# Residual rows summed in memory by an accumulating scatter, and the first norm taken tile by tile, in a hybrid encoder step on one core

## The chip, the cores and the metric

The kernel runs on one core of one Trainium2 chip. The metric is device time in microseconds (us) of one execution, the median of several runs. Times inside an execution are counted from the start of the span, which runs from the first to the last instruction that the profiler records.

## The reference

One layer of a streaming encoder is applied to 304 tokens: 16 meta tokens and 256 prompt tokens (one stream) and 32 sample tokens (another stream). All data are float32, rows have 2048 elements. What matters here:

```python
x = x + mix @ w_out                      # the mixer (RG-LRU and mLSTM branches), on rmsnorm(x)
xf = rmsnorm(x)                          # 304 rows of 2048
g_idx = argmax(xf @ w_rg + b_rg)         # one of 4 groups for each token
top_v, top_i = top_k(e_logits[g_idx], 2) # two of its 4 experts; top_w: softmax times p(group)
for e in range(16):
    hdn = silu(xf @ w_g[e]) * (xf @ w_u[e])           # 2048 -> 512
    out = out + gates[:, e:e + 1] * (hdn @ w_d[e])    # 512 -> 2048
y = rmsnorm(x + out)
```

## The kernel before

**Start.** Five DMAs issued by ScalarE (`load_x`) bring x into three tiles of up to 128 tokens: meta tokens and the first 112 prompt rows (tile 0), 128 prompt rows (tile 1), the last 16 prompt rows and the 32 sample rows (tile 2, 48 rows). All five count on one semaphore `x_loaded`; SyncE (which then starts to stream weights) and ScalarE (which then squares the tiles, L1003) wait for all five. VectorE turns the sums into means, ScalarE takes the root (L1006), VectorE scales the tiles (L1370), TensorE turns them (L659, L650), ScalarE and VectorE split them into a rounded part and its rest (L1017, L1380), and TensorE begins the first of 104 products with slices of `w_in` (L665 to L667). Ahead of it TensorE runs `WARM` matmuls (L655), whose results nothing reads. Every weight matrix is split into a rounded part (ScalarE, L1011) and a rest (VectorE, L1375), and a product is three matmuls for each of its steps.

**Routing.** After the mixer, x with its residual stands in `xtok`, the normed rows are stored in memory (`xn2_rows`). VectorE chooses experts and gives each (token, expert) a slot: each expert has 64 slots (`CAP`), filled from the first one, and 16 experts make 1024 slots, one round. GpSimd scatters each token's number into `slot_token` at its two slots (L1976); the table was filled with zeros at the start, so that an empty slot names token 0.

**Expert loop.** It runs over eight pairs of experts (the first partly ahead of the loop, the last behind it). Weights come in units of 2 MB into a ring of four slots, issued by SyncE when TensorE has finished with a slot (`groups_done`); ScalarE rounds them (L1237), VectorE takes the rest (L1788), TensorE multiplies (L904, L905, and L931 to L933 for the down product). GpSimd's function `store` does for each pair, in this order: the index column of the next pair's slots (`gidx`, L1994), the gather of their rows (L1996), then for each of the two experts a wait for its result and its store into `slot_out` (L2005). It waits for both stores, frees `ysb`, and goes on to the next pair. VectorE copies a result out of PSUM in four pieces (`results_out`, L1818).

**End.** When all is stored, GpSimd gathers for each of the three tiles its two result rows per token (L2020, six gathers). VectorE multiplies them by the weights `w1` and `w2` and adds them to x (`take`, L1875 and L1878), ScalarE squares (L1326) and takes the root (L1328), VectorE scales (`scaled`, L1889), SyncE stores the outputs (L604).

```python
v.wait_ge(groups_done, p(12, G_MOE + s + 1))    # results_out
if e == 0:
    v.wait_ge(y_free, p(1, 1))
```

## Time and profile before

| | us |
|---|---|
| median of three runs | 1998.38 (1995.9 to 1998.81) |
| profiled execution, its own time | 2001.61 |
| its span | 2000.1 |
| mean granted clock of TensorE | 0.976 of full speed |
| busy: TensorE, VectorE, ScalarE, GpSimd | 1879.3, 1241.1, 1005.1, 100.9 |

The busy times are sums over the whole span; the stages have different limits, so the rows below are taken from single stages. In a timeline a row gives the start and the length of an instruction (of several, where a count stands behind it), and in square brackets how long its engine had been idle before it and what ended that. Matmuls are pipelined, so their ends are modelled.

### The profile page before, as it was taken

What the parts mean: (1) busy time and instruction counts of PE and PEld (TensorE: products, weight loads), DVE (VectorE), ACT (ScalarE), POOL (GpSimd) and SP (SyncE); (2) the same over time, 40 slices, a digit from 0 to 9 for tenths busy, and PEclk for the clock granted to TensorE, in tenths of its full rate; (3) what the DMA queues carried; (4) which work ended last, traced back from release to release, by engine and by line L of the source; (5) the groups of instructions that cost most, each with busy time, mean ns of one, the idle gap of its engine ahead of it and who ended that gap; (6) DMA issues with size and microseconds to landing.
All of it is one profiled execution on the core that took longest, in us unless ns stands there. A gap on an engine that the chain in (4) does not pass through costs nothing.

```text
span 2000.1 us, 28137 instructions
## 1 busy us (share of the span) xinstructions
PE 1879.3 (94%) x11723; PEld 1679.6 (84%) x11723; DVE 1241.1 (62%) x1437; ACT 1005.1 (50%) x999; POOL 100.9 (5%) x188
## 2 busy tenths in 40 slices
PE   6999999999999999999999999999988989898981
PEld 5999999999999999999999999998666666666650
DVE  4764634547645445664343445444799999999984
ACT  5333644653334433453334333333678787878761
POOL 3001011000000000000000000000100000000001
PEclk8999999999999999999999999999999999999996
DMA  6555554545444444445565675546599999999975
GB/s 165 160 155 139 148 143 126 144 128 146 121 123 132 118 133 132 122 119 166 150 166 150 171 194 159 157 127 240 230 375 421 399 411 398 419 394 410 402 305 157
DMA packets 379167, 422.83 MB, mean 211 GB/s; under 512 B 13823, under 2 KB 358747, under 8 KB 362969
## 3 DMA queue, kind: packets, MB, share of 16 engines
q1 hardware_dynamic: 369849, 385.55, 59.0%
q0 software_dynamic: 7504, 29.75, 4.2%
q10 hardware_dynamic: 1712, 6.04, 1.0%
q8 instruction: 80, 1.31, 0.3%
q14 instruction: 22, 0.18, 0.0%
HBM read 405.87 MB, written 15.45 MB: 211 GB/s over the span
## 4 chain that ended last, share of the span: by engine, by line
PE 79%; DMA 10%; DVE 5%; issue 3%; ACT 3%; ACTq 0%; POOL 0%; DVEq 0%; POOLq 0%; SPq 0%
PE bank L629 17%; PE bank L631 16%; PE bank L630 16%; DMA ring<-in_w_exp_gate 5%; DMA ring<-in_w_exp_down 4%; PE bank L931 3%; PE bank L932 3%; PE bank L933 3%; PE bank L685 3%; PE bank L789 2%; PE bank L791 2%; PE bank L790 2%; ACT w_high L1237 1%; DVE w_low L1788 1%; PE bank L737 1%
## 5 line engine op out<-in xcount | busy, mean ns | idle before, releaser
L1375 DVE TENSOR_TENSOR low<-ring,high 128x2048 fp32r<-128x2048 f32 x172 | 394.1, 2291 | 566.0 <-ACT high L1011 565.7
L629 PE MATMUL bank<-x_high,high 128*128 128x304 f32 x2160 | 662.6, 307 | 0.0
L631 PE MATMUL bank<-x_high,low 128*128 128x304 f32 x2160 | 652.0, 302 | 0.0
L1011 ACT ACTIVATE high<-ring 128x2048 fp32r<-128x2048 f32 x172 | 329.1, 1913 | 533.5 <-DMA ring<-in_w_in 317.8
L630 PE MATMUL bank<-x_low,high 128*128 128x304 f32 x1904 | 572.1, 300 | 0.0
L1788 DVE TENSOR_TENSOR w_low<-ring,w_high 128x2048 fp32r<-128x2048 f32 x192 | 430.8, 2284 | 22.2 <-ACT w_high L1237 21.4
L1237 ACT ACTIVATE w_high<-ring 128x2048 fp32r<-128x2048 f32 x192 | 363.3, 1922 | 98.0 <-DMA ring<-in_w_exp_gate 33.5
L629 PEld LDWEIGHTS bank<-x_high,high 128*128 128x128 f32 x2160 | 405.9, 188 | 5.0 <-issue 3.3
L631 PEld LDWEIGHTS bank<-x_high,low 128*128 128x128 f32 x2160 | 406.1, 188 | 0.0
L630 PEld LDWEIGHTS bank<-x_low,high 128*128 128x128 f32 x1904 | 358.5, 188 | 1.4
L904 PE MATMUL bank<-w_high,xs 128*128 128x512 f32 x512 | 210.5, 411 | 28.1 <-DVE xs L1799 12.4
L905 PE MATMUL bank<-w_low,xs 128*128 128x512 f32 x512 | 202.3, 395 | 0.0
L904 PEld LDWEIGHTS bank<-w_high,xs 128*128 128x128 f32 x512 | 97.2, 190 | 72.3 <-DVE w_low L1788 34.6
L630 PE MATMUL bank<-hb_rounded,high 128*128 128x304 f32 x512 | 154.8, 302 | 0.0
L931 PE MATMUL bank<-w_high,hs_high 128*64 128x512 f32 x256 | 104.8, 409 | 25.8 <-DVE hs_low L1810 25.8
L905 PEld LDWEIGHTS bank<-w_low,xs 128*128 128x128 f32 x512 | 97.4, 190 | 18.4
L932 PE MATMUL bank<-w_high,hs_low 128*64 128x512 f32 x256 | 104.2, 407 | 0.0
L933 PE MATMUL bank<-w_low,hs_high 128*64 128x512 f32 x256 | 103.9, 406 | 0.0
L630 PEld LDWEIGHTS bank<-hb_rounded,high 128*128 128x128 f32 x512 | 96.3, 188 | 0.0
L931 PEld LDWEIGHTS bank<-w_high,hs_high 128*64 128x64 f32 x256 | 35.9, 140 | 57.0 <-issue 35.3
L629 PE MATMUL bank<-ym_high,high 128*128 128x304 f32 x256 | 77.7, 303 | 0.0
L631 PE MATMUL bank<-ym_high,low 128*128 128x304 f32 x256 | 77.5, 303 | 0.0
(372 smaller groups left out, 2145.3 us busy)
## 6 DMA issues: line engine op xcount, KB each, us to landing
ring<-in_w_in SPq DMA_DIRECT2D x120, 1024.0 KB, 5.6
ring<-in_w_exp_gate SPq DMA_DIRECT2D x32, 2048.0 KB, 9.2
ring<-in_w_exp_up SPq DMA_DIRECT2D x32, 2048.0 KB, 10.9
ring<-in_w_exp_down SPq DMA_DIRECT2D x32, 2048.0 KB, 11.0
ring<-in_w_proj_rnn SPq DMA_DIRECT2D x20, 1024.0 KB, 6.1
ring<-in_w_proj_mlstm SPq DMA_DIRECT2D x16, 1024.0 KB, 6.1
ring<-in_w_out SPq DMA_DIRECT2D x16, 1024.0 KB, 6.1
slot_out<-HB POOLq DMA_DIRECT2D x16, 512.0 KB, 8.4
```

The costliest lines, as they stand in the source:

```text
L629: pe.matmul(dst, hi[:, k, :], rhs_high(k), start=(k == 0), stop=False)
L630: pe.matmul(dst, hi[:, k, :], rhs_low(k), start=False, stop=False)
L631: last = pe.matmul(dst, lo[:, k, :], rhs_high(k), start=False, stop=(k == KD - 1))
L904: pe.matmul(dst, xs[:, kk, e, :], w_hi[:, k, :], start=(kk == 0), stop=False)
L905: last = pe.matmul(dst, xs[:, kk, e, :], w_lo[:, k, :], start=False, stop=(kk == KD - 1))
L931: pe.matmul(dst, h_hi, w_hi[:, b, :], start=(k == 0), stop=False)
L932: pe.matmul(dst, h_lo, w_hi[:, b, :], start=False, stop=False)
L933: last = pe.matmul(dst, h_hi, w_lo[:, b, :], start=False, stop=(k == KE - 1))
L1011: act.activation(high[n % 4], raw[n % 4], ACT.Copy).then_inc(t_split, 1)
L1237: act.activation(w_high[(2 * q + c) % 4], half(w_raw[s % 4], c), ACT.Copy).then_inc(w_split, 1)
L1375: v.tensor_tensor(low[n % 4], raw[n % 4], high[n % 4].bitcast(F32), ALU.subtract).then_inc(t_rest, 1)
L1788: v.tensor_tensor(half(w_low[s % 4], c), half(w_raw[s % 4], c), w_high[(2 * q + c) % 4].bitcast(F32), ALU.subtract).then_inc(w_rest, 1)
```

## The change

Two things are changed together.

The first is where the experts' results are summed. x is stored in memory (`x_rows`) by SyncE once the mixer is done. The slot table gets a second word: beside the token's number its weight, so its scatters wait until VectorE has made `w1` and `w2`. Empty slots name token 304, which is out of bounds, and gathers and scatters leave such rows out. In the loop GpSimd loads, behind the gather of the next pair, the index and weight column of the pair at hand (`sidx`). VectorE multiplies each result by its weight as it takes it out of PSUM, for which it waits until `sidx` is there. GpSimd adds the rows of a result to `x_rows` by an indirect DMA that accumulates; the second expert's add waits until the first one's is done. At the end SyncE loads the three tiles of `x_rows` back; the six gathers and the six multiply-adds are gone.

The second is the start. Each tile of x has its own semaphore, and ScalarE squares a tile when it has landed. A root on a word that nothing reads stands ahead of the squares. `WARM` goes from 24 to 8, and 2, 2 and 6 matmuls whose results nothing reads follow the transposes of the three tiles.

The diff, without the declarations of semaphores:

```diff
     xn2_rows = nc.dram_tensor("xn2_rows", (T, DM), F32)
-    slot_token = nc.dram_tensor("slot_token", (SLOTS + P, 1), I32)
-    slot_out = nc.dram_tensor("slot_out", (SLOTS, DM), F32)
+    slot_token = nc.dram_tensor("slot_token", (SLOTS + P, 2), I32)
+    x_rows = nc.dram_tensor("x_rows", (T, DM), F32)
     ctx = ExitStack()
...
         kc = sb("kc", [P, NE + EG])
-        tokid = sb("tokid", [P, 3], I32)
+        tokw = sb("tokw", [P, 2, 3, 2], I32)
+        tokw_f = tokw[:, :, :, :].bitcast(F32)
+        sidx = sb("sidx", [CAP, 2, 2], I32)
+        sidx_f = sidx[:, :, :].bitcast(F32)
         nrounds = sb("nrounds", [P, 2], I32)
         slot_i = sb("slot_i", [P, 2, 3], I32)
-        gidx = sb("gidx", [P, 1], I32)
+        gidx = sb("gidx", [P, 2], I32)
         SQ_GROUPS = [(0, 4), (4, 8), (8, 12), (12, 14), (14, 16)]
...
         diag8 = sb("diag8", [NH, 2 * NH])[:, :]
-        zeros_i = sb("zeros_i", [P, (SLOTS + P) // P], I32)
+        no_token = HBf[:, 2 * BW + 4 * P:2 * BW + 4 * P + (SLOTS + P) // P * 2].bitcast(I32)
         x2t = [AB[:, :, :].rearrange("p a b -> p (a b)")[:, j * T:(j + 1) * T] for j in range(4)]
...
         y1 = xntok
-        y2 = HBf[:, 0:HALF].rearrange("p (a b) -> p a b", a=3)
         nbf = OGf[:, DM:2 * DM]
...
         NVEC, NPAR = 11, 3
-        WARM = 24
+        WARM, KEEP = 8, (2, 2, 6)
         RG0 = [18 + 9 * g for g in range(G)]
...
+        X_PARTS = (2, 1, 2)
...
                 return w[:, :, c * P:(c + 1) * P]
-            sp.wait_ge(x_loaded, 16 * 5)
+            for i in range(3):
+                sp.wait_ge(x_loaded[i], 16 * X_PARTS[i])
             for n in range(G_MOE):
...
             sp.dma_start(nbf, bcast(A["norm_f_w"])).then_inc(nbf_loaded, 16)
+            sp.wait_ge(x2_ready, KD)
+            for i, (t, n) in enumerate(TT):
+                sp.dma_start(x_rows[t:t + n, :], xtok[0:n, i, :]).then_inc(x2_stored, 16)
             sp.wait_ge(rounds_ready, 1)
...
                 wait_apart(sp, rounds_ready, slot_full[b], n * (NPAIR * 3 * 16) + LOADS_MOE[b] * 16)
+            wait_apart(sp, rounds_ready, y_stored, n * (NPAIR * 32))
+            for i, (t, m) in enumerate(TT):
+                sp.dma_start(xtok[0:m, i, :], x_rows[t:t + m, :]).then_inc(xf_loaded[i], 16)
+
             for i, (r, p0, n) in enumerate([(0, NM, P - NM), (P - NM, 0, P), (2 * P - NM, 0, PL)]):
...
                         last.then_inc(x_transposed, 1)
+                for _ in range(KEEP[i]):
+                    pe.matmul(bank[0][:, 0:P], ones[:, :], before[:, :], start=True, stop=True)
             pe.wait_ge(t_rest, 1)
...
                 split = [(0, NM, P - NM), (P - NM, 0, P), (2 * P - NM, 0, PL)]
-                act.dma_start(xtok[0:NM, 0, :], A["meta_tokens"]).then_inc(done, 16)
+                act.dma_start(xtok[0:NM, 0, :], A["meta_tokens"]).then_inc(done[0], 16)
                 for i, (r, p0, n) in enumerate(split):
-                    act.dma_start(xtok[p0:p0 + n, i, :], A["x_prompt"][0, r:r + n, :]).then_inc(done, 16)
-                act.dma_start(xtok[PL:NL, 2, :], A["x_sample"][0]).then_inc(done, 16)
+                    act.dma_start(xtok[p0:p0 + n, i, :], A["x_prompt"][0, r:r + n, :]).then_inc(done[i], 16)
+                act.dma_start(xtok[PL:NL, 2, :], A["x_sample"][0]).then_inc(done[2], 16)
             load_x(x_loaded)
...
                     act.dma_start(xtok[r0:r1, 2, X2C:DM], rows_[:, X2C:DM]).then_inc(xr_loaded, 16)
-            act.wait_ge(x_loaded, 16 * 5)
             act.wait_ge(ss_init, 1)
+            act.activation(small[:, 18:19], small[:, 18:19], ACT.Sqrt)
             for i, (t, n) in enumerate(TT):
+                act.wait_ge(x_loaded[i], 16 * X_PARTS[i])
                 act.activation(junk[0:n], xtok[0:n, i, :], ACT.Square, accum_out=small[0:n, i:i + 1]).then_inc(ss_done, 1)
...
                 split(n + 2)
+                if n == 2 * KR:
+                    act.wait_ge(zeroed, 16)
                 evac(n - 1)
...
             for i, (t, n) in enumerate(TT):
-                act.wait_ge(fin_ss, i + 1)
+                act.wait_ge(xf_loaded[i], 16)
                 act.activation(y1[0:n, i, :], xtok[0:n, i, :], ACT.Square, accum_out=small[0:n, 18 + i:19 + i]).then_inc(fin_sq, 1)
...
                     v.wait_ge(y_free, p(1, 1))
+                    v.wait_ge(sidx_loaded, p(16, 16))
                 for b in range(4):
-                    last = v.tensor_copy(ysb[0:CAP, e, b * DE:(b + 1) * DE], bank[b][0:CAP, 0:DE])
+                    last = v.tensor_scalar(ysb[0:CAP, e, b * DE:(b + 1) * DE], bank[b][0:CAP, 0:DE],
+                                           sidx_f[:, e, 1:2], None, ALU.mult)
                 last.then_inc(y_out, 1)
...
             step(v.tensor_tensor(w2, ex, w1, ALU.mult))
+            v.tensor_copy(tokw_f[:, 0, :, 1:2], w1)
+            v.tensor_copy(tokw_f[:, 1, :, 1:2], w2).then_inc(tokw_ready, 1)
             rest_unit(first, 1, 1)
...
             pair(lambda m, c: tail * m + c, False)
-            def take(i, c):
-
-                t, n = TT[i]
-                v.wait_ge(y_loaded[i][c], 16)
-                if c == 0:
-                    step(v.scalar_tensor_tensor(out=xtok[0:n, i, :], in0=y1[0:n, i, :], scalar=w1[0:n, i, :],
-                                                in1=xtok[0:n, i, :], op0=ALU.mult, op1=ALU.add))
-                else:
-                    v.scalar_tensor_tensor(out=xtok[0:n, i, :], in0=y2[0:n, i, :], scalar=w2[0:n, i, :],
-                                           in1=xtok[0:n, i, :], op0=ALU.mult, op1=ALU.add).then_inc(fin_ss, 1)
-
             def mean(i):
...
             v.wait_ge(nbf_loaded, 16)
-            take(0, 0)
-            take(0, 1)
-            take(1, 0)
             mean(0)
-            take(1, 1)
+            mean(1)
             scaled(0)
-            take(2, 0)
-            mean(1)
-            take(2, 1)
+            mean(2)
             scaled(1)
-            mean(2)
             scaled(2)
...
             pool.memset(ones[:, :], 1.0)
-            pool.memset(zeros_i[:, :], 0)
+            pool.memset(no_token, T)
             for e in range(NE):
...
             step(pool.memset(trl[0:PL, PL:NL], NEG))
-            pool.iota(tokid[:, :], pattern=[[P, 3]], base=0, channel_multiplier=1)
+            for c in range(2):
+                pool.iota(tokw[:, c, :, 0], pattern=[[P, 3]], base=0, channel_multiplier=1)
             pool.affine_select(out=ident[:, :], in_=ident[:, :], compare_op=ALU.not_equal, fill=1.0, base=0,
...
             pool.wait_ge(consts_ready, 1)
-            pool.dma_start(slot_token.rearrange("(p c) o -> p (c o)", p=P), zeros_i[:, :]).then_inc(zeroed, 16)
+            pool.dma_start(slot_token.rearrange("(p c) o -> p (c o)", p=P), no_token).then_inc(zeroed, 16)
             pool.wait_ge(vec_ready, 1)
...
             pool.wait_ge(rounds_ready, 1)
+            pool.wait_ge(tokw_ready, 1)
             for c in range(2):
...
                     pool.indirect_dma_start(out=slot_token[:, :], out_offset=bass.IndirectOffsetOnAxis(ap=slot_i[0:n, c, i:i + 1], axis=0),
-                                            in_=tokid[0:n, i:i + 1], in_offset=None).then_inc(perm_written, 16)
+                                            in_=tokw[0:n, c, i, :], in_offset=None).then_inc(perm_written, 16)
             pool.wait_ge(perm_written, 16 * 6)
             pool.wait_ge(xn2_stored, 16 * 3)
+            pool.wait_ge(x2_stored, 16 * 3)
+            last_row = pool.to_reg(T - 1)
             nr = pool.value_load(nrounds[0:1, 1:2], min_val=1, max_val=MAXR)
             tail = pool.value_load(nrounds[0:1, 0:1], min_val=NPAIR - 1, max_val=MAXR * NPAIR - 1)
-
-            with pool.If(nr > 1):
-                step(pool.memset(HBf[:, 2 * DM:3 * DM], 0.0))
-                with pool.Fori(0, (SLOTS - ROUND_ROWS) // P) as k:
-                    pool.dma_start(slot_out[bass.ds(k * P + ROUND_ROWS, P), :], HBf[:, 2 * DM:3 * DM]).then_inc(rest_zeroed, 16)
-                pool.wait_ge(rest_zeroed, (SLOTS - ROUND_ROWS) // P * 16)
-            with pool.Else():
-                pool.nop()
             def gather(p, p1):
...
                 pool.indirect_dma_start(out=rows, out_offset=None, in_=xn2_rows[:, :],
-                                        in_offset=bass.IndirectOffsetOnAxis(ap=gidx[:, :], axis=0)).then_inc(rows_gathered, 16)
+                                        in_offset=bass.IndirectOffsetOnAxis(ap=gidx[:, 0:1], axis=0),
+                                        bounds_check=last_row, oob_is_err=False).then_inc(rows_gathered, 16)
             pool.sem_inc(y_free, 1)
...
                     gather(p + 1, p + 2)
+                pool.dma_start(sidx[:, :, :], slot_token[bass.ds(p * P, P), :].rearrange("(e c) o -> c e o", e=2)).then_inc(sidx_loaded, 16)
                 for e in range(2):
-                    pool.wait_ge(y_out, p * 2 + (e + 2))
-                    pool.dma_start(slot_out[bass.ds(p * P + e * CAP, CAP), :], ysb[0:CAP, e, :]).then_inc(y_stored, 16)
+                    if e == 0:
+                        pool.wait_ge(y_out, p * 2 + 2)
+                    else:
+                        first_stored, second_out = pool.to_reg(p * 32 + 16), pool.to_reg(p * 2 + 3)
+                        pool.wait_ge(rounds_ready, 1)
+                        pool.wait_ge(y_stored, first_stored)
+                        pool.wait_ge(y_out, second_out)
+                    pool.sem_inc(adds_begun, 1)
+                    pool.indirect_dma_start(out=x_rows[:, :], out_offset=bass.IndirectOffsetOnAxis(ap=sidx[:, e, 0:1], axis=0),
+                                            in_=ysb[0:CAP, e, :], in_offset=None, bounds_check=last_row, oob_is_err=False,
+                                            compute_op=ALU.add).then_inc(y_stored, 16)
                 pool.wait_ge(y_stored, p * 32 + 32)
...
             wait_apart(pool, rounds_ready, rows_gathered, tail * 16)
-            wait_apart(pool, rounds_ready, xs_ready[1], nr * NPAIR)
-            wait_apart(pool, rounds_ready, groups_done, nr * (NPAIR * 12) + G_MOE)
-
-            def results(table):
-                for i, (t, n) in enumerate(TT):
-                    for c, dst in enumerate((y1, y2)):
-                        pool.indirect_dma_start(out=dst[0:n, i, :], out_offset=None, in_=table,
-                                                in_offset=bass.IndirectOffsetOnAxis(ap=slot_i[0:n, c, i:i + 1], axis=0)).then_inc(y_loaded[i][c], 16)
-            with pool.If(nr > 1):
-                results(slot_out[:, :])
-            with pool.Else():
-                results(slot_out[0:ROUND_ROWS, :])
             pool.wait_ge(cn_stored, 32 * NH)
```

## Rows read from the trace of the kernel before

**Rows 1.** Start, timeline: start us, us, engine, line, operation, [idle before <-releaser]

```profile
1.51 1.40 ACTq L986 DMA_DIRECT2D XG<-in_x_prompt  x3
...
12.50 1.91 ACT L1003 ACTIVATE HB<-XG 128x2048 f32<-128x2048 f32 x1 [7.58 <-DMA XG<-in_x_sample]
...
14.73 7.17 PE L655 MATMUL bank<-before,ones 128*128 128x128 f32 x48 [0.69 <-DVE vec L1360]
...
18.85 1.28 ACT L1006 ACT_TABLE_LOAD   x1 [0.28 <-DVE small L1350]
...
20.59 4.28 DVE L1370 TENSOR_SCALAR XG<-XG,small 128x2048 f32<-128x2048 f32 x3
...
27.66 0.38 PE L665 MATMUL bank<-x_high,high 128*128 128x304 f32 x1 [2.10 <-DVE x_low L1380]
...
47.20 13.71 SPq L540 DMA_DIRECT2D ring<-in_w_in  x3
```

**Rows 2.** Start, windows: us; PE, PEld, DVE, ACT, POOL busy; clock; DMA share; GB/s

```profile
25.00:28.00 3.00, 0.90 (x9) 0.80 (x10) 3.00 (x4) 2.72 (x7) 2.69 (x6) 1.00 1.20 289
28.00:32.00 4.00, 4.00 (x17) 2.90 (x15) 3.40 (x8) 2.95 (x4) 4.00 (x9) 0.53 0.95 174
...
60.00:100.00 40.00, 40.00 (x289) 40.00 (x288) 28.83 (x52) 14.18 (x19) 0.00 (x0) 1.00 0.59 159
```

**Rows 3.** Expert loop, one pair of experts, windows (columns as above)

```profile
1497.00:1564.00 67.00, 60.36 (x273) 42.03 (x272) 63.03 (x47) 53.28 (x41) 2.69 (x4) 0.97 0.98 406
```

**Rows 4.** Timeline of GpSimd, ahead of and inside the expert loop

```profile
1402.10 2.41 POOL L1976 DMA_INDIRECT slot_token<-tokid,slot_i  x1 [10.72 <-DVE nrounds L1781]
...
1410.69 0.88 POOL L1976 DMA_INDIRECT slot_token<-tokid,slot_i  x1 [0.30 <-issue]
1417.75 0.57 POOL L1994 DMA_DIRECT2D gidx<-slot_token  x1 [6.18 <-PE bank L880]
...
1498.51 0.54 POOL L2005 DMA_DIRECT2D slot_out<-HB  x1 [35.14 <-DVE HB L1818]
1508.22 0.58 POOL L1994 DMA_DIRECT2D gidx<-slot_token  x1 [9.17 <-issue]
1515.15 1.01 POOL L1996 DMA_INDIRECT HB<-xn_rows,gidx  x1 [6.35 <-DMA gidx<-slot_token]
```

**Rows 5.** DMA view of six pairs (kind, count, KB, median us to landing)

```profile
slot_out<-HB POOLq DMA_DIRECT2D x12, 512.0 KB, 8.4
gidx<-slot_token POOLq DMA_DIRECT2D x6, 0.5 KB, 5.8
HB<-xn_rows,gidx POOLq DMA_INDIRECT x6, 12.1
```

**Rows 6.** Timeline of VectorE, ahead of and inside the expert loop

```profile
1420.50 0.16 DVE L1858 TENSOR_TENSOR OG<-OG 128x3 f32<-128x3 f32 x1
...
1459.59 2.47 DVE L1818 COPY HB<-bank 64x512 f32<-64x512 f32 x4
...
1526.66 2.47 DVE L1818 COPY HB<-bank 64x512 f32<-64x512 f32 x4
```

**Rows 7.** Chain of waits at the end (start us, us, what)

```profile
1959.19 4.11 DMA slot_out<-HB
```

**Rows 8.** Timeline of the end, ScalarE and VectorE

```profile
1976.45 1.91 ACT L1326 ACTIVATE XG<-XG 128x2048 f32<-128x2048 f32 x1 [29.46 <-DVE XG L1878]
...
1979.04 0.20 ACT L1328 ACTIVATE small<-small 128x1 f32<-128x1 f32 x1 [0.58 <-DVE small L1883]
...
1993.51 2.34 DVE L1889 SCALAR_TENSOR_TENSOR XG<-XG,small,OG 48x2048 f32<-48x2048 f32 x1
```

**Rows 9.** DMA view of the first 40 us (kind, count, KB, us to landing)

```profile
XG<-in_x_prompt ACTq DMA_DIRECT2D x1, 1024.0 KB, 8.6
XG<-in_x_prompt ACTq DMA_DIRECT2D x1, 896.0 KB, 5.6
XG<-in_x_sample ACTq DMA_DIRECT2D x1, 256.0 KB, 9.5
```

More of the change, by code:

```diff
@@ L412, in build @@
         y_free = sem("y_free")
-        x_loaded = sem("x_loaded")
+        x_loaded = [sem(f"x_loaded{i}") for i in range(3)]
+        X_PARTS = (2, 1, 2)
         ss_init = sem("ss_init")
@@ L443, in build @@
         silu_done = sem("silu_done")
-        fin_ss = sem("fin_ss")
         fin_sq = sem("fin_sq")
@@ L450, in build @@
         xr_loaded = sem("xr_loaded")
-        y_loaded = [[sem(f"y_loaded{i}_{c}") for c in range(2)] for i in range(3)]
+        xf_loaded = [sem(f"xf_loaded{i}") for i in range(3)]
+        x2_stored = sem("x2_stored")
+        tokw_ready = sem("tokw_ready")
+        sidx_loaded = sem("sidx_loaded")
+        adds_begun = sem("adds_begun")
         fin_out = sem("fin_out")
@@ L457, in build @@
         perm_written = sem("perm_written")
-        rest_zeroed = sem("rest_zeroed")
         idx_loaded = sem("idx_loaded")
```

## The prediction

> **What bounds the kernel now.** I read the granted clock and the windows by stage first, then the timeline of the two ends, then the DMA view and the timeline of GpSimd inside the expert loop, because the diff touches just these places.
>
> The start runs in series. ScalarE idles 7.58 us until the last of five x transfers has landed, squares three tiles back to back, loads a second activation table (1.28 us) for the root, and VectorE scales from 20.59; the first product starts at 27.66 and its ring slot is free at 47.20 [rows 1]. So the first product takes 19.5 us. TensorE is only 0.30 busy from 25 to 28, and from 28 on the granted clock is 0.5, the lower level of 1.2 GHz [rows 2]. From 60 to 100 TensorE is busy all the time [rows 2], so whatever the first product gains, everything behind it inherits.
>
> In the expert loop (one pair of experts in 67 us) two things are nearly full: VectorE at 63.03 of 67.00 us, and the DMA engines at a share of 0.98 [rows 3]. A third thing is nearly tight: GpSimd's relay. The second result of a pair is stored at 1498.51, the next index column is requested at 1508.22, the gather is issued at 1515.15 [rows 4] and lands 12.1 us later [rows 5], at 1527.3; the first result of the next pair leaves PSUM at 1526.66 [rows 6]. The reader is to see that this relay has no slack.
>
> The end is in series again: the last store is issued at 1959.19 and lands in 4.11 [rows 7]; six gathers and six multiply-adds follow, and the last scaling starts at 1993.51 [rows 8].
>
> **The change, part by part.**
>
> *Start.* By their issue (1.51 for the first prompt tile [rows 1], 0.45 apart) and times to landing (5.6, 8.6, 9.5 [rows 9]) the three tiles land at 7.1, 10.6 and 12.4. A square takes 1.91 and some 0.2 more for its sum. Tile 0 is then done at 9.2, tile 1 at 12.7, tile 2 at 14.8, where before three squares in a row from 12.50 [rows 1] end at 18.5: 3.7 us earlier. The root's table is loaded by a dummy root while x is in flight, and Square needs none of its own: at the end Square and root follow one another with 0.58 idle, too little for a 1.28 load [rows 8]. That takes off 1.3. Sum 5.0. VectorE then scales from 15.6 to 20.0. The weight chunk that is next is requested at 12.5 as before and lands by 18.1 if it takes the 5.6 of tile 0, so it does not hold this back. First product at 22.7. Bounds: 1.3 if the tiles land together, 5.0 as worked out.
>
> *Warm-up and clock.* Warm-up falls from 48 records (7.17 us, 0.149 each [rows 1]) to 16: 2.4 us, ending at 17.1, where the first transposes now start. Ten matmuls (20 records, 3.0 us) go between and behind the transposes; 1.8 of it lies ahead of the first product, in a stretch that waits for VectorE anyway, so they cost nothing. What they buy: TensorE is hardly idle from 14.7 to 22.7, where before it was 0.30 busy just ahead of the drop [rows 2]. If the clock holds, the first product shrinks. At the low clock its 16 steps take 19.5 us. At full speed I estimate 0.42 for three matmuls (three times the 0.138 by which 289 follow one another in 40 us [rows 2]) and 0.45 to 0.75 for three transposes in nine of the steps: 10.8 to 13.5 us, a gain of 6 to 8.7; I take 7. Bounds 0 (clock falls all the same) and 8.7.
>
> *Ahead of the loop.* SyncE stores x (2.5 MB) before it waits for the routing; it has nothing else queued until the first slot frees. GpSimd's six scatters of the slot table, issued from 1402.10, now wait for the weights w1, w2, ready after 1420.50 [rows 4, 6], 19 us later. The last of the six went out at 1410.69 [rows 4], 8.6 after the first, so now at about 1430. The index request then moves from 1417.75 to about 1433, the gather to 1440, landing 1452, the new index-and-weight load at about 1455; its first reader stands at 1459.59 [rows 6]. Hidden, with 4 us of cover. Without that cover the first pair pays what it lacks, once.
>
> *Loop.* Copy out of PSUM becomes multiply out of PSUM: same size, same pass, nothing. Dropped slots shrink traffic: 304 tokens twice over 16 experts fill 38 of 64 slots. Three things act on the relay:
> - The add takes the store's place. 64 rows stored take 8.4, 128 rows gathered 12.1 [rows 5]: 3.7 for 64 more rows, 4.7 fixed. An add reads its target too, so it lies between 4.7 + 2.2 = 6.9 (38 rows, reading free) and 12.1 (64 more moves). I take 10.2, +1.8; descriptor work (1.01 for a gather against 0.54 for a store [rows 4]) +0.5.
> - The gather with 76 rows of 128 lies between 9.1 and 12.1. Slots fill from the front, so some engines keep all their rows; I take 11.1, -1.
> - The new load of index and weight is issued behind the gather, on GpSimd's queue, in 128 pieces like the index column (5.8 [rows 5]). It lands between 0 and 5.8 after the gather; I take 3. VectorE now waits for it before the first result, and behind that instruction stand all its weight splits, for which TensorE waits.
>
> Relay now: 1498.51 to 1527.3 is 28.8; after 28.8 + 1.8 + 0.5 - 1 + 3 = 33.1 against 28.2 at which VectorE arrives: a stall of 4.9 per pair. VectorE's idle time of 4.0 per pair [rows 3] and the DMA engines' 0.02 take up some 3.5 of it, leaving 1.4 in each of seven pairs: 10 us. Low end: 6.9, 9.1 and 0 give no stall, and the saved bytes (0.85 MB beside 25.2 MB of weights, by their shapes) at most 1 us in each of eight pairs, -8. High end: 12.1, 12.1 and 5.8 give 38.8, a stall of 10.6, +7 in seven pairs, +50.
>
> The Trainium skill says, in Collectives: The Full Stack, section "The bandwidth ceiling", that an add inside a DMA reads two sources through one ring and moves at half the rate of a copy. No adding DMA is in this trace, so nothing here agrees or disagrees. By that rule the add is the 12.1 of my bound, the stall 6.8 and the loop +23.
>
> *End.* Add instead of store: 0.5 more to issue, landing 4.11 [rows 7] to 12.1; nothing else is on the engines, so I take 5.5. It has landed at 1964.7 (before 1963.3). SyncE then loads x: tile 0 after 5.6, tile 1 after 8.6, tile 2 after 9.5 [rows 9]: 1970.9, 1974, 1975. Square to root is 2.8 per tile [rows 8], so roots at 1973.8, 1977, 1980; three scalings of 2.34 on VectorE, of which the first waits for the second tile's mean at 1976.8, end at 1984.9. Before: 1993.51 + 2.34 = 1995.85. The output behind it is the same. Gain 11; with an add of 12.1, 4.5; with 4.11, 12.4.
>
> **Sum.** The profiled execution took 2001.6 around its span of 2000.1; the median of the runs shown is 1998.4. -5 -7 +10 -11 = -13: 1988.6 by the profiled execution, 1985 by the median.
>
> **Rivals.**
> 1. *The clock falls in the first product all the same.* For it: steps with transposes mixed in have a thinner matmul stream, and a cut warm-up. Against it: no idle stretch is left. Gain 16 - 10 = 6: 1992. The Trainium skill (TensorE: Matmul & The Clock Gate, Part 1) holds that the throttled state is the default and activity lifts it, which speaks against a shorter warm-up: the low clock would then stand from the first transposes on. The trace has the clock full after one length of warm-up [rows 2] and no other, so it neither agrees nor disagrees.
> 2. *The relay becomes the bound* (slower). The index load stands in full behind the gather and the add costs a gather: 28.8 + 3.7 + 0.5 - 1 + 5.8 = 37.8, stall 9.6, about +6 in seven pairs, +42; against 23 from the ends, net +19: 2017. It decides from a stall of 3.5 + 23/7 = 6.8 per pair on. For it: no slack today. Against it: a waiting loop has emptier DMA queues, so these transfers shorten.
> 3. *No stall at all.* Dropped rows really shorten gather and add, the index load comes with the gather: loop -5, net -28: 1970.
> 4. *The squares don't start early*, tiles landing together: 3.7 less, a case within the first range; the separate times to landing [rows 9] speak against it.
>
> **Chances.** Forecast 0.45 (own range 1976 to 1996), rival 1 0.20, rival 2 0.20, rival 3 0.15. A measurement here can tell 0.2%, 4 us, from no change. Faster: 0.43 + 0.15 + 0 + 0.15 = 0.73; same 0.02 + 0.03 + 0.02 = 0.07; slower 0.20. The range of 1968 to 2010 leaves out most of rival 2 and a little of rival 3.
>
> **What would show it.** Start: root at 15 instead of 20, first product at 23, granted clock 1 up to 48, ring slot free by 35. Loop: VectorE's multiply out of PSUM idle before it, waiting for the index load, 2 to 8 us in each pair from the second on; time from one first result to the next 67 before, 68 to 69 after. End: from the issue of the last add (a store at 1959.19 today) to the end of the span 30 us instead of 40.9. The prediction is wrong if the add lands in over 12 us, if the loop's pitch passes 70, or if the clock drops in the first product.

## The result, and the profile after

The changed kernel takes 2057.31 us (median of four runs, 2056.48 to 2063.73) against 1998.6 for the kernel before on the same chip: a ratio of 1.029, 95% interval 1.0256 to 1.0324. It is slower by 59 us, where 1985 us was forecast with 0.73 for faster. The profiled execution took 2063.73 us, its span 2062.2, at a mean granted clock of 0.964.

The start went much as forecast. The timeline of ScalarE after (start us, us, engine, line, operation, idle before):

```profile
7.27 1.91 ACT L1019 ACTIVATE HB<-XG 128x2048 f32<-128x2048 f32 x1 [2.07 <-DMA XG<-in_x_prompt]
...
11.25 1.91 ACT L1019 ACTIVATE HB<-XG 128x2048 f32<-128x2048 f32 x1 [1.98 <-DMA XG<-in_x_prompt]
...
13.28 1.91 ACT L1019 ACTIVATE HB<-XG 48x2048 f32<-48x2048 f32 x1
...
15.58 0.21 ACT L1022 ACTIVATE small<-small 128x3 f32<-128x3 f32 x1 [0.29 <-DVE small L1368]
```

Each square begins as its tile lands, and no table load stands ahead of the root, which comes at 15.58 (forecast 15; before 20.1, behind the table load of [rows 1]). The first slot of the weight ring is free at 36.51 (forecast 35; 47.20 in [rows 1]), and TensorE begins the first product at 24.08 (forecast 22.7; 27.66 in [rows 1]):

```profile
24.08 0.39 PE L680 MATMUL bank<-x_high,high 128*128 128x304 f32 x1
```

The windows view of after shows the clock held, and a loop that is not full any more:

```profile
28.00:32.00 4.00, 4.00 (x25) 3.18 (x24) 4.00 (x6) 2.41 (x6) 3.09 (x6) 1.00 1.28 250
1510.00:1577.00 67.00, 46.79 (x204) 33.35 (x202) 49.34 (x39) 41.60 (x33) 17.47 (x5) 0.87 0.78 314
```

The first row answers to the 0.53 of [rows 2]. The second answers to [rows 3]: VectorE is busy for 49.34 of 67 us instead of 63.03, the DMA engines 0.78 instead of 0.98. No engine and no queue is nearly full any more, so they wait for one another. Only GpSimd has more to do, 17.47 instead of 2.69. Its timeline in one pair, after:

```profile
1487.50 15.84 POOL L2015 DMA_INDIRECT x_rows<-HB,sidx  x1 [26.21 <-DVE HB L1837]
1513.33 0.62 POOL L1995 DMA_DIRECT2D gidx<-slot_token  x1 [9.98 <-issue]
1519.62 1.06 POOL L1997 DMA_INDIRECT HB<-xn_rows,gidx  x1 [5.67 <-DMA gidx<-slot_token]
1520.66 0.68 POOL L2005 DMA_DIRECT2D sidx<-slot_token  x1
1535.67 7.18 POOL L2015 DMA_INDIRECT x_rows<-HB,sidx  x1 [14.32 <-DVE HB L1837]
```

These rows answer to [rows 4]. The instruction that issues the second expert's add holds GpSimd for 15.84 us, where the store's took 0.54; the first expert's for 7.18. The waits of VectorE from 1510 to 1915 us (us in total, times, longest):

```profile
DVE HB L1837 <- DMA sidx<-slot_token: 81.2, 5, 17.0
```

In each of five pairs the multiply out of PSUM waits some 16 us for the index-and-weight load. From one first add to the next (1454.14, then 1535.67, ... to 2006.15 in the eighth pair) the pitch is 78.9 us on average instead of 67. What the DMA view of after says of the transfers themselves (median us from issue to landing) answers to [rows 5]:

```profile
x_rows<-HB,sidx POOLq DMA_INDIRECT x10, 19.8
gidx<-slot_token POOLq DMA_DIRECT2D x5, 1.0 KB, 5.7
HB<-xn_rows,gidx POOLq DMA_INDIRECT x5, 12.0
sidx<-slot_token POOLq DMA_DIRECT2D x5, 1.0 KB, 11.4
```

The 19.8 counts from the instruction's start and so holds the wait on GpSimd. The gather lands as late as before (12.0 against 12.1).

Where the 62.1 us between the two spans are, by the issue of results and adds:

| stage | forecast | measured |
|---|---|---|
| start (the start alone, first experiment) | -12 | -12.4 |
| from there to the first result | 0 | +3.8 |
| eight pairs | +10 | +83.5 |
| last issue to the end (40.9 before, 28.1 after) | -11 | -12.8 |
| sum | -13 | +62.1 |

What ends the long instruction? VectorE's timeline of after beside the two adds of one pair (1535.67 to 1542.85, and 1569.06 to 1584.90):

```profile
1532.13 2.72 DVE L1837 TENSOR_SCALAR HB<-bank,sidx 64x512 f32<-64x512 f32 x4 [17.02 <-DMA sidx<-slot_token]
1534.77 6.68 DVE L1806 TENSOR_TENSOR w_low<-ring,w_high 128x2048 fp32r<-128x2048 f32 x3
1541.38 1.40 DVE L1817 TENSOR_TENSOR xs<-bank,xs 128x256 fp32r<-128x256 f32 x4
...
1568.09 15.48 DVE L1806 TENSOR_TENSOR w_low<-ring,w_high 128x2048 fp32r<-128x2048 f32 x7
1583.50 0.41 DVE L1824 TENSOR_TENSOR XG<-XG,bank 128x256 f32<-128x256 f32 x1
```

Both adds end 1.3 to 1.4 us after VectorE leaves a back-to-back run of weight subtractions (L1806, both operands in SBUF) for an operation that takes an operand from PSUM. And 1.42 us is what the last add of the kernel takes (at 2034.05), when VectorE has nothing left to do. That gives **theory 1**: the run holds GpSimd's indirect instruction until it is broken. **Theory 2**: the accumulating transfer, or making its descriptors, is slow in itself. **Theory 3**: the stall comes from the index load's place behind the gather.

### The profile page after: what moved, and what is told of

Read it like the earlier page. It is cut to its first block, busy times and chain, and to the rows that moved or that the text cites. A ratio compares the mean times of both kernels' runs of the same rounds, so it can differ in the third digit from the quotient of the medians.

```text
span 2062.2 us, 28129 instructions
## 1 busy us (share of the span) xinstructions
PE 1874.2 (91%) x11711; PEld 1681.7 (82%) x11711; DVE 1228.4 (60%) x1433; ACT 1005.0 (49%) x999; POOL 259.4 (13%) x191
## 4 chain that ended last, share of the span: by engine, by line
PE 71%; DMA 15%; DVE 8%; issue 4%; POOL 1%; ACT 1%; POOLq 0%; SPq 0%; DVEq 0%; ACTq 0%
PE bank L642 16%; PE bank L644 16%; PE bank L643 16%; DMA x_rows<-HB,sidx 7%; DMA sidx<-slot_token 4%; DVE w_low L1806 3%; PE bank L700 3%; DMA gidx<-slot_token 2%; PE bank L804 2%; PE bank L806 2%; PE bank L805 2%; PE bank L946 2%; PE bank L947 2%; PE bank L948 2%; DVE HB L1837 2%
## 5 line engine op out<-in xcount | busy, mean ns | idle before, releaser
L1806 DVE TENSOR_TENSOR w_low<-ring,w_high 128x2048 fp32r<-128x2048 f32 x192 | 428.0, 2281 | 10.5 <-ACT w_high L1255 10.3
L919 PE MATMUL bank<-w_high,xs 128*128 128x512 f32 x512 | 212.3, 415 | 20.1 <-DVE w_low L1806 14.2
L2015 POOL DMA_INDIRECT x_rows<-HB,sidx x16 | 166.0, 10372 | 315.2 <-DVE HB L1837 299.4
L907 PE MATMUL bank<-ident,HB 128*128 128x128 f32 x112 | 24.7, 412 | 100.1 <-DVE HB L1837 100.1
L1837 DVE TENSOR_SCALAR HB<-bank,sidx 64x512 f32<-64x512 f32 x64 | 43.5, 736 | 111.8 <-DMA sidx<-slot_token 101.2
L907 PEld LDWEIGHTS bank<-ident,HB 128*128 128x128 f32 x112 | 22.2, 220 | 103.0 <-issue 103.0
```

The source lines that it names most:

```text
L919: pe.matmul(dst, xs[:, kk, e, :], w_hi[:, k, :], start=(kk == 0), stop=False)
L1806: v.tensor_tensor(half(w_low[s % 4], c), half(w_raw[s % 4], c), w_high[(2 * q + c) % 4].bitcast(F32), ALU.subtract).then_inc(w_rest, 1)
L2015: pool.indirect_dma_start(out=x_rows[:, :], out_offset=bass.IndirectOffsetOnAxis(ap=sidx[:, e, 0:1], axis=0), in_=ysb[0:CAP, e, :], in_off ...
```

## Experiments

**1. The start alone.** The kernel before with the start's hunks of the diff and nothing else.

> The kernel before with the start of the change alone: x in three parts, a square as each tile lands, the root's table asked for early, warm-up of 16 records with products kept going between the transposes. All theories: the first result is multiplied out of PSUM about 9 us earlier (that is what the changed kernel's trace shows at its first add, 1454.14 against 1462.78), the pitch stays 67 us, the end stays 40.9 us, so the total falls by 8 to 11 us, 0.4 to 0.55%: about 1989 us where the kernel before takes 1998.6. If the loop swallowed the head's gain (its start being set by something else), no change.

1988.4 us against 1999.61, ratio 0.994 (0.992 to 0.996). The first store stands at 1449.93 (1462.78 before), the span is 12.4 us shorter (the medians are 11.2 apart). The loop hands the gain on undiminished.

**2. VectorE steps aside.**

```diff
                     results_out(p, 13, 1)
+                    v.wait_ge(adds_begun, p(2, 2))
+                    for j in range(24):
+                        v.memset(pad[:, j:j + 1], 0.0)
                     rest_unit(p, 15, 15)
```

> The changed kernel, but after each pair's second result VectorE waits until GpSimd has come to the second add and then sets 24 single columns (about 1.5 to 2.5 us with no operand read from SBUF) before its next subtraction. Theory 1 (VectorE's unbroken run of subtractions with both operands in SBUF holds the add's instruction on GpSimd): the second add takes 1.4 to 3 us instead of 15.84, the first still about 7.2; the stall at the multiply falls from 17.0 to 2 to 4 us, pitch 67 to 70 us instead of 80 to 82, total 1975 to 1995 us. Theory 2 (the adding transfer's own descriptor work is slow): the second add still takes about 15 us, the pitch is 81 us or some 2 more, total 2057 to 2075 us. Theory 3 (the index load behind the gather makes the stall): second add as short as in theory 1 or not, the stall stays above 10 us.

1994.82 us, ratio 0.9971 (0.9956 to 0.9987): of the 83.5 us that the loop had lost, 67.0 are gone (from the first issue to the last 512.9 us, where it was 579.9 and before the change 496.4), with an edit that takes nothing from the add. GpSimd and VectorE in one pair of it:

```profile
1558.99 3.22 POOL L2019 DMA_INDIRECT x_rows<-HB,sidx  x1 [26.21 <-DVE HB L1838]
1571.50 0.61 POOL L1999 DMA_DIRECT2D gidx<-slot_token  x1 [9.29 <-issue]
```

```profile
1558.30 0.33 DVE L1866 MEMSET pad<- 128x1 f32 x24 [0.21 <-POOLq L2018]
1558.61 13.30 DVE L1807 TENSOR_TENSOR w_low<-ring,w_high 128x2048 fp32r<-128x2048 f32 x6
```

The second add falls from 15.84 to 3.22, the first stays at 7.17: the numbers of theory 1, but not quite its reason. By these rows the sets are over before the add begins, and the add ends at 1562.21, within the second of six subtractions that follow one another without a pause. This run let the add through unbroken; how it differs from the runs of the changed kernel stands in the last section. The pitch is 69.4 on average, the wait for the index load 17.2 us in four pairs instead of 81.2 in five.

**3. A plain scatter.** `compute_op=ALU.add` taken out, so rows are overwritten.

> The changed kernel with the scatter writing its rows instead of adding them (this leaves out the sum with the residual). Theory 1: an indirect write is held just as an indirect add is, 7.2 and 15.8 us on GpSimd in every pair, pitch 79 to 82 us, total within 10 us of the changed kernel's 2057. Theory 2 (adding makes it slow): both instructions fall to about 1 to 1.5 us, pitch about 67 to 70, total under 1995 us. Landing of the transfer beyond the hold: 6 to 8.4 us instead of 8.9.

2042.98 us (one run); on GpSimd 6.6 us for the first scatter and 15.3 for the second, each in six of the eight pairs. Adding makes no difference of this size, theory 2 falls. One pair is an experiment of its own. GpSimd there:

```profile
1725.49 4.29 POOL L2015 DMA_INDIRECT x_rows<-HB,sidx  x1 [26.78 <-DVE HB L1837]
```

It got through after 4.29, in the midst of a run in which the third subtraction began at 1728.96, 2.25 us behind the second where the others follow at 2.20: ScalarE's rounding, for which it waits, had ended 0.03 us before. The next first scatter came 70.0 us after this pair's, instead of some 80.

**4. A direct store.** The indirect add becomes `pool.dma_start(x_rows[e * CAP:(e + 1) * CAP, :], ysb[0:CAP, e, :])`: fixed rows, no sum.

> The changed kernel with a direct store of each result to fixed rows of the residual in place of the indirect add (this leaves out the sum and the destination rows). Theory 1 (what is held is the instruction that makes its descriptors from an index list): 0.54 us on GpSimd in the midst of the same run of subtractions, pitch 67 to 70 us, total 1970 to 1995 us; the index load and the gather stand in the same order, so the stall at the multiply is then what those two alone make, 0 to 4 us. Theory 3 (the index load behind the gather): stall above 10 us per pair as before, total above 2040.

1980.45 us (one run), pitch 67.2. GpSimd and VectorE in one pair:

```profile
1556.49 0.54 POOL L2015 DMA_DIRECT2D x_rows<-HB  x1 [35.51 <-DVE HB L1837]
```

```profile
1555.72 13.28 DVE L1806 TENSOR_TENSOR w_low<-ring,w_high 128x2048 fp32r<-128x2048 f32 x6
```

A direct store is issued in 0.54 us while the same run goes on, and with the index load and gather in their old order the multiply waits 7.2 us in all. Only the indirect form is held.

**5. One operand instead of two.** The split is left out: the low part holds the whole weight.

```diff
-                v.tensor_tensor(half(w_low[s % 4], c), half(w_raw[s % 4], c),
-                                w_high[(2 * q + c) % 4].bitcast(F32), ALU.subtract).then_inc(w_rest, 1)
+                v.tensor_scalar(half(w_low[s % 4], c), half(w_raw[s % 4], c), 1.0, 0.0, ALU.mult, ALU.add,
+                                accum_out=pad[:, 2 * q + c:2 * q + c + 1]).then_inc(w_rest, 1)
```

> The changed kernel in which VectorE's subtractions for the low parts of the weights (two operands in SBUF) become a product of the one raw operand with 1, with its sum written out; this leaves the split out, so the low part holds the whole weight. Count, place and size stay. Theory 1 (two SBUF operands hold the add): both adds take 1.4 to 2 us on GpSimd in the midst of the same back-to-back run, the stall falls to 0 to 3 us and the pitch to 67 to 70 us if the operation lasts 2.2 us as the subtraction does. Its rival within theory 1 (any unbroken run on VectorE holds it): 7 and 15 us as before, pitch about 81. Theory 2 (the add is slow in itself): the same 7 and 15 us.

1984.41 us (one run), pitch 68.0. GpSimd, VectorE beside the last of these adds, and VectorE's group from 1510 to 1915 us (busy us, mean ns):

```profile
1520.37 1.52 POOL L2016 DMA_INDIRECT x_rows<-HB,sidx  x1 [15.27 <-DVE HB L1838]
1553.80 1.45 POOL L2016 DMA_INDIRECT x_rows<-HB,sidx  x1 [31.91 <-DVE HB L1838]
...
1726.39 1.50 POOL L2016 DMA_INDIRECT x_rows<-HB,sidx  x1 [16.38 <-issue]
```

```profile
1726.29 2.27 DVE L1807 TENSOR_SCALAR_CACHE_REDUCE w_low<-ring 128x2048 fp32r<-128x2048 f32 x1
```

```profile
L1807 DVE TENSOR_SCALAR_CACHE_REDUCE w_low<-ring 128x2048 fp32r<-128x2048 f32 x143 | 319.2, 2276 | 11.6 <-ACT w_high L1256 11.2
```

As many operations, as long (2276 ns each) and as close together, but with one operand in SBUF: both adds go through in 1.5 us. It is not VectorE's being busy that holds the add, it is the second SBUF operand. A 78 ns read of the sum overlaps the end of each operation, so the runs are not the same in every respect; but it is not this read that lets the add through, since the add at 1726.39 begins and ends within one operation (1726.29 to 1728.56).

**6. The index load first.** The `sidx` load moves ahead of the gather and its index column.

> The changed kernel with the load of index and weight issued ahead of the index column and the gather, right behind the second add's landing. Theory 1 (the held add): the multiply is released at 15.8 + 8.9 + 0.7 + 5.5 = 31 us after the second add begins, about 1 us late, but the gather still begins 15.8 - 1.4 = 14.4 us late by the hold, and what waits is then TensorE for the gathered rows: a part of the 17 us moves there, pitch 72 to 79 us, total 2010 to 2045 us. Theory 3 (the index load's place behind the gather made the stall): pitch 67 to 69, total below 1990 us.

2042.39 us, ratio 1.02 (1.0155 to 1.0245). The second add is held as before (15.8 us). In five pairs the gather now meets the run behind the first result and is held for 8.2 to 8.8 us, although it adds nothing, and the first add behind it takes only 1.51. GpSimd and VectorE in one of them:

```profile
1589.90 8.33 POOL L1997 DMA_INDIRECT HB<-xn_rows,gidx  x1 [6.26 <-DMA gidx<-slot_token]
1598.53 1.51 POOL L2015 DMA_INDIRECT x_rows<-HB,sidx  x1 [0.30 <-issue]
```

```profile
1590.60 6.68 DVE L1806 TENSOR_TENSOR w_low<-ring,w_high 128x2048 fp32r<-128x2048 f32 x3
```

The multiply now waits 15.2 us in five pairs (from 1510 to 1915 us), and the waits of TensorE there show where the rest went:

```profile
PE bank L907 <- DMA HB<-xn_rows,gidx: 67.0, 5, 15.4
```

The pitch is 76.4. Theory 3 falls: the order decides who waits, not that somebody waits.

**7. A gap between the subtractions.** One single-column `memset` behind each subtraction, no waiting.

> The changed kernel with one single-column set (no operand read; 24 of them took 0.33 us) behind each of VectorE's weight subtractions; 31 to 32 per pair, about 0.5 to 2 us of VectorE. Theory 1, in the form that the hold lasts until the run of subtractions has a gap: both adds end at most one subtraction and the free add behind their start, 1.4 to 3.7 us, instead of 7.2 and 15.84; pitch 68 to 71 us, total 1985 to 2010 us. If a gap so small lets nothing through: 7.2 and 15.84 as before, pitch 79 or more, total 2055 to 2075 us.

2063.36 us, ratio 1.0294 (1.0249 to 1.0338): the miss among these runs. The first add still took 7.2 us in six pairs of the eight, the second 15.9 in five. The two that were held for less (13.69 and 11.47, in the first two pairs) ended 1.3 us behind the start of a subtraction that had waited for ScalarE's rounding, not behind a set. The sets (59 ns each) lie within the times of the subtractions around them, so no gap comes about. Theory 1 must be put more narrowly: an instruction between two subtractions is not enough.

**8. The gather ahead.** The held add is accepted, and the gather for the pair after next is issued in GpSimd's free time between a pair's adds.

```diff
+            pool.wait_ge(rows_t_done, 1)
+            gather(1, 2)
             def store(p, more):
-                if more:
-                    pool.wait_ge(rows_t_done, p + 1)
-                    gather(p + 1, p + 2)
...
                     else:
+                        if more:
+                            pool.wait_ge(rows_t_done, p + 2)
+                            gather(p + 2, p + 3)
```

> The changed kernel with the gather for the pair after next issued between a pair's two adds, where GpSimd has nothing to do, instead of behind the second. The adds stay as they are. Theory 1 (the held add): the instructions still take 7.2 and 15.8 us, but behind the second add there is only its landing and the index load: 15.8 + 8.9 + 0.6 + 5.5 = 30.8 us, against 67.0 - 33.4 = 33.6 us from one second add to the next first one, of which the multiply and its handing over take 3.5. So the stall at the multiply falls from 17.0 to 0 to 1.5 us, pitch 67 to 68.5 us, and the ends' 8.6 and 12.8 us show: 1977 to 1990 us. Theory 2 (the adding transfer is slow in itself and loads the DMA rings): the gather beside the adds lands later, TensorE waits for its rows, pitch above 72, total above 2010 us.

1986.44 us, ratio 0.9931 (0.9908 to 0.9954): faster than the kernel before by 0.7%. GpSimd in one pair of it, and VectorE beside the gather and the second add:

```profile
1522.98 7.11 POOL L2017 DMA_INDIRECT x_rows<-HB,sidx  x1 [19.25 <-DVE HB L1837]
1529.61 1.09 POOL L1995 DMA_DIRECT2D gidx<-slot_token  x1
1541.50 2.94 POOL L1997 DMA_INDIRECT HB<-xn_rows,gidx  x1 [10.80 <-DMA gidx<-slot_token]
1556.36 4.86 POOL L2017 DMA_INDIRECT x_rows<-HB,sidx  x1 [11.91 <-DVE HB L1837]
1570.36 0.66 POOL L2004 DMA_DIRECT2D sidx<-slot_token  x1 [9.14 <-DMA x_rows<-HB,sidx]
```

```profile
1541.24 11.09 DVE L1806 TENSOR_TENSOR w_low<-ring,w_high 128x2048 fp32r<-128x2048 f32 x5
...
1555.38 4.47 DVE L1806 TENSOR_TENSOR w_low<-ring,w_high 128x2048 fp32r<-128x2048 f32 x2
1560.16 6.70 DVE L1806 TENSOR_TENSOR w_low<-ring,w_high 128x2048 fp32r<-128x2048 f32 x3 [0.30 <-ACT w_high L1255]
```

The first add is held as long as ever and it costs nothing. The second, expected at 15.8, is held for 4.85 to 4.87 in six pairs of eight: VectorE pauses for 0.30 us at 1559.85, waiting for ScalarE, and the add is done 1.37 after that. The gather met five subtractions in an unbroken row as well, but was held only to the end of the first: it ended at 1544.44, 1.0 us after the second had begun. From 1510 to 1915 us VectorE waits no more for `sidx`. Pitch 67.7.

**9. Both mends.** The gather ahead and VectorE stepping aside.

> Both mends together: the gather issued between the adds, and VectorE stepping aside for the second add. Theory 1: with the gather ahead the hold of the second add is covered, so stepping aside buys nothing more and costs VectorE 0.5 us per pair: pitch within 1 us of the gather moved alone, total 0 to 7 us above it. If the hold still reached the path there (the index load landing behind the multiply's time), this one is 5 us or more faster than the gather moved alone.

1985.49 us, ratio 0.9921 (0.9901 to 0.9941) beside 0.9931 (0.9908 to 0.9954): no difference that can be told. With the gather ahead the hold is off the path.

**10 to 12. The two halves of the start,** on top of the gather ahead, which ran again beside them.

> The gather between the adds once more, as the base for the two runs of the start: 0.993 of the kernel before, pitch 67.7 us.

1988.42 us, ratio 0.9937 (0.9914 to 0.9959). Then `KEEP = (0, 0, 0)`:

> The gather between the adds, without the ten matmuls that keep TensorE going between and behind the first transposes. If those matmuls are what holds the clock, the granted clock in the first product is 0.5 again, the product takes 6 to 8.7 us longer and so does the whole: 0.3 to 0.45% above the same kernel with them. If the early squares alone close the idle stretch, the clock stays 1 and the time is the same within 1 us.

1997.38 us, ratio 0.9985 (0.997 to 1.0001): 9.0 us are given back. Its windows show why (TensorE's busy time is the first one, the clock the third number from the end):

```profile
20.00:24.00 4.00, 2.20 (x17) 1.79 (x15) 4.00 (x7) 3.23 (x8) 3.69 (x9) 0.87 1.19 290
24.00:28.00 4.00, 4.00 (x16) 2.80 (x14) 3.00 (x7) 2.43 (x3) 4.00 (x8) 0.50 1.17 297
```

TensorE is busy 2.20 of the four us in which the clock begins to fall, and it then stays at its lower level to 40 us, as before the change. And the squares late, with the matmuls kept: ScalarE waits for all three tiles, and the early root is taken out.

> The gather between the adds, with all x tiles awaited ahead of the first square and the root's table loaded behind them, as before; the matmuls between the transposes stay. If the start's gain is the sum of two terms (5.0 us by the squares and the table, 7 by the clock), this costs 5 us, 0.25%, with the clock at 1; if TensorE's wait for VectorE lets the clock fall all the same, it costs 11 to 13 us.

1996.45 us, ratio 0.9976 (0.9956 to 0.9995): 8.0 us given back, not 5 and not 11. VectorE scales from 22.64 instead of 15.61, 7.0 later. 1.28 of that is an activation table that ScalarE loads at 13.24, ahead of the first square but behind the waits; in the kernel before, a table load stands at 3.63, while x is in flight, so this term is the experiment's own. The clock falls to 0.50 only from 24 to 28 us, behind four us in which TensorE ran nothing (0.00 busy from 20 to 24), and is full from 32 on.

## Why the prediction was wrong

**The step that failed** is the first of the loop's three terms: "descriptor work (1.01 for a gather against 0.54 for a store) +0.5". It measured 15.84 against 0.54, +15.3, in every pair but those in which VectorE paused. The relay from the issue of the second result, step by step:

| | before | forecast | after |
|---|---|---|---|
| to the request of the next index column | 9.7 | 12.0 | 25.8 |
| to the gather's issue | 6.9 | 6.9 | 6.3 |
| to the last landing that the multiply waits for | 12.1 | 14.1 | 12.5 |
| sum | 28.8 | 33.1 | 44.6 |

VectorE arrives at 28.2, so 44.6 makes a stall of 16.4 (the longest measured is 17.0), less some 3.5 absorbed 12.9, times seven pairs 90; 83.5 were lost. The frame held, with its stall, its absorption and its seven pairs, and one entry was wrong by a factor of 30.

The price had been read from a row in which nothing was held: the gather of 1.01 us in [rows 4] began within 0.02 us of the start of a subtraction (the first row of VectorE here). But another pair of the same trace has this one on GpSimd and the other two on VectorE:

```profile
1784.01 3.01 POOL L1996 DMA_INDIRECT HB<-xn_rows,gidx  x1 [7.00 <-DMA gidx<-slot_token]
```

```profile
1515.13 2.34 DVE L1788 TENSOR_TENSOR w_low<-ring,w_high 128x2048 fp32r<-128x2048 f32 x1
...
1783.85 2.29 DVE L1788 TENSOR_TENSOR w_low<-ring,w_high 128x2048 fp32r<-128x2048 f32 x1
1786.57 4.50 DVE L1788 TENSOR_TENSOR w_low<-ring,w_high 128x2048 fp32r<-128x2048 f32 x2 [0.42 <-ACT w_high L1237]
```

Held until the subtraction ends at 1786.14, then 0.9 us of its own. With this row the term would have been +2.5 and the loop, by the prediction's own sum, +24 instead of +10: a warning, but not yet the hold over seven subtractions. For that the trace of before has no row, since only direct stores are issued right behind a result there. The add is issued right behind a result, and there VectorE has the subtractions lined up that the result held back: the worst place for it.

The Trainium skill (SBUF — State Buffer, section "Who interferes with whom") says that a VectorE instruction with two inputs in SBUF contends with a GpSimd instruction that reads SBUF. It calls the ports that they share an exclusive lock and says, of VectorE's modes that take them for one operand, that whoever issues first has them for its whole instruction and the other is blocked. Experiment 5 agrees on the operands. On the length, the 3.01 us above and the 2.94 of the gather in experiment 8 agree with a hold for one instruction; the 15.84 us, over seven subtractions of 2.27, do not. The page also tells of a probe in which `tensor_tensor` did not stall a DMA; here it did.

**What held.** With the hold gone, by one operand, the kernel took 1984.41 us against 2001.04 for the kernel before in the same set, -16.6 where -13 was forecast: its loop from the first issue to the last is 503.4 us against 496.4, +6.9 where +10 was forecast. So the hold is the whole of the error, within what one run can tell.

- *Start, -5.0 and -7.* Measured together -12.4: right. By the rows of the changed kernel the first product begins 3.6 us earlier, not 5.0, and its slot is free 12.4 us later instead of 19.5, which is -7.1. Most of what the first part lacks are the ten matmuls, which were to cost nothing: without them the first product begins at 22.85, with them at 23.93 (experiments 11 and 10). Undone one at a time the two halves cost 9.0 and 8.0 us, together more than the whole gain, so each needs the other. Rival 1 did not come about, and rival 4 neither.
- *Ahead of the loop, hidden with 4 us of cover.* Wrong by 7.6 us, so the cover was short by 3.6: the first multiply waits 3.60 us at 1450.58. The six scatters of the slot table took 1.80 to 2.65 us each, where the later ones took 0.88 to 0.97 in the kernel with the start alone. In the changed kernel they run beside the weight subtractions.
- *Add's landing 10.2.* In the pair shown, 24.72 less 15.84 is 8.9 behind the instruction; with one operand an add landed 10.5 us after its issue. Right. The same rows scattered without adding (experiment 3) land 7.5 us behind the held second instruction, the adds 7.9 (medians of six), so adding costs some 0.4 us here; 38 more rows at the prediction's 3.7 for 64 would be 2.2. The half rate of the Trainium skill (Collectives: The Full Stack, section "The bandwidth ceiling"), which the prediction put at 12.1, is not seen here.
- *Gather, -1.* Nothing: 12.0 against 12.1. Left-out rows bought no time.
- *Index load, 3 behind the gather.* 0.5: the gather lands 12.0 after 1519.62, the load at 1532.1.
- *Multiply for copy, nothing.* 736 ns against 675 on average from 1510 to 1915 us: 0.06 x 64 is 3.9 us in all, on the engine that is the bound when nothing is held.
- *End, -11.* -12.8; the last add landed in 5.55 (forecast 5.5).

Rival 2, the relay as the bound, is what happened, with the chance of 0.20 that it had, but not by the landings from which it was priced: +19 was said, +59 came about. "The prediction is wrong if the loop's pitch passes 70" was the right gauge: it read 78.9.

**The better kernel** is the change with the gather ahead: 0.9931 and 0.9937 of the kernel before in two sets of runs. The start alone makes 0.994, so the scatter part, mended, has bought nothing that can be told. By spans its end is 12 us shorter (28.8 after the last issue), its loop 4.6 longer, and its first result 5.0 later than with the start alone.

## What to carry to other kernels

The duration of an instruction that makes a transfer from a list of indices is no property of the transfer: look for all its occurrences in the trace, and at what VectorE ran beside the longest. Before swapping a direct DMA for an indirect one, ask which operations with two SBUF operands will run back to back where it is issued, and who stands in line behind it on its queue. In this kernel the long holds were all in runs that began right behind an operation out of PSUM. Where the hold can't be taken away, move the work that queues behind it: that was worth as much as taking it away.

## What the runs showed of the hardware that was not expected

- A run of two-operand VectorE instructions can hold an indirect DMA instruction of GpSimd over all of them (15.84 us, seven subtractions), not over one. Pauses of 0.30 us (experiment 8) and 0.17 us (the seventh pair of the changed kernel, where the second add took 11.43) let it through. Sets of 59 ns between the subtractions did not (experiment 7).
- How long the hold lasts goes with how the run begins, in the traces of every kernel here but that of experiment 5. An indirect instruction that met a run beginning directly behind an operation out of PSUM was held to the run's end or to a subtraction that had waited for ScalarE (135 of 136 that had two subtractions or more before them). One that met a run beginning behind a pause, or behind operations on SBUF alone, got through at the latest at the end of the one subtraction that it met, though up to six more followed without a gap (all of 95). The 24 sets of experiment 2 stand between the multiply and the run and so make it one of the second kind, with 3.22 us; the sets of experiment 7 leave it one of the first. Why the beginning decides stays open, as does what in the indirect instruction needs VectorE to stop; that it is the read of its index list was not tried.
- The stall took TensorE's granted clock along: 0.87 over the 67 us of one pair, where it was 0.97. How much of the 83.5 us is this was not separated.
- A plain indirect scatter costs GpSimd 0.90 us with VectorE idle (the last one of experiment 3), the accumulating one 1.42: adding costs half a microsecond, waiting for VectorE fourteen.
